# Fetching the blocks for a seven-product matrix multiply from ScalarE's queue instead of GpSimd's

## What is computed

```python
def _swiglu(x, w_gate, w_up, w_down):
    return (jax.nn.silu(x @ w_gate) * (x @ w_up)) @ w_down

h = _rmsnorm(x, ffn1_norm[layer])
x = x + 0.5 * _swiglu(h, ffn1_w_gate[layer], ffn1_w_up[layer], ffn1_w_down[layer])
```

## Time and profile before

| | us |
|---|---|
| median of 3 runs | 2193.39 (2192.85 to 2194.36) |
| profiled execution, its own time | 2189.33 |
| span of its trace | 2187.6 |
| PE busy | 2072.6 (95%) |
| DVE busy | 1447.6 (66%) |
| ACT busy | 1184.1 (54%) |
| POOL busy | 930.6 (43%) |

### The profile page before, as it was taken

One profiled execution on the slowest core, in us unless ns is written; L12 is line 12 of the kernel. 1 busy time (PEld: TensorE's weight loads), 2 busy tenths in 40 slices (PEclk: granted clock), 3 DMA queues, 4 the chain that ended last, 5 costly groups with the idle time before them and its releaser, 6 DMA issues.

```text
span 2187.6 us, 35091 instructions
## 1 busy us (share of the span) xinstructions
PE 2072.6 (95%) x11738; PEld 1800.8 (82%) x11738; DVE 1447.6 (66%) x2525; ACT 1184.1 (54%) x2186; POOL 930.6 (43%) x709
## 2 busy tenths in 40 slices
PE   8999999899999989889999899999999998989998
PEld 6878888798888879888887788888878887988886
DVE  6597854787652377776258789899777348767523
ACT  4566653566642356665244467777655335666422
POOL 2233451755643275664327701201254317565431
PEclk9999999999999999999999999999999999999999
DMA  5323263445533245554324422222454434555331
GB/s 172 109 93 94 78 221 90 151 173 180 184 116 96 78 151 173 174 169 130 98 86 165 125 68 81 77 78 83 131 177 159 154 96 135 192 173 173 124 96 67
DMA packets 83027, 282.78 MB, mean 129 GB/s; under 512 B 9225, under 2 KB 9481, under 8 KB 82417
## 3 DMA queue, kind: packets, MB, share of 16 engines
q1 hardware_dynamic: 51120, 182.08, 26.8%
q0 software_dynamic: 20096, 72.18, 9.9%
q10 hardware_dynamic: 11712, 27.27, 3.3%
HBM read 261.03 MB, written 18.89 MB: 128 GB/s over the span
## 4 chain that ended last, share of the span: by engine, by line
PE 57%; issue 15%; DVE 12%; POOL 11%; ACT 2%; DMA 2%; POOLq 1%; SPq 0%; DVEq 0%; ACTq 0%
PE bank L188 15%; PE bank L190 15%; PE bank L189 15%; PE bank L195 2%; PE bank L194 2%; POOL s_raw L817 2%; DMA w_raw<-stream 2%; POOL s_holes L817 2%; DVE w_lo L162 2%; POOL s_raw L818 2%; POOL s_holes L818 2%; PE bank L2226 1%; POOL s_holes L820 1%; POOL s_raw L820 1%; DVE t_lo L674 1%
## 5 line engine op out<-in xcount | busy, mean ns | idle before, releaser
L162 DVE TENSOR_TENSOR w_lo<-w_raw,w_hi 128x1024 fp32r<-128x1024 f32 (+1 forms) x337 | 464.0, 1392 | 332.0 <-ACT w_hi L157 329.1
L157 ACT ACTIVATE w_hi<-w_raw 128x1024 fp32r<-128x1024 f32 (+1 forms) x337 | 330.9, 984 | 387.7 <-PE bank L190 227.5
L188 PE MATMUL bank<-xn_hi,w_hi 128*128 128x512 f32 (+1 forms) x1192 | 434.8, 365 | 7.4 <-DVE h L670 4.0
L190 PE MATMUL bank<-xn_hi,w_lo 128*128 128x512 f32 (+1 forms) x1192 | 420.2, 353 | 0.0
L189 PE MATMUL bank<-xn_lo,w_hi 128*128 128x512 f32 (+1 forms) x1192 | 419.4, 352 | 0.0
L188 PEld LDWEIGHTS bank<-xn_hi,w_hi 128*128 128x128 f32 x1192 | 226.5, 190 | 38.9 <-DVE h L670 5.2
L190 PEld LDWEIGHTS bank<-xn_hi,w_lo 128*128 128x128 f32 x1192 | 226.0, 190 | 30.8
L189 PEld LDWEIGHTS bank<-xn_lo,w_hi 128*128 128x128 f32 x1192 | 226.6, 190 | 28.1 <-issue 2.6
L188 PE MATMUL bank<-t_hi,s_hi 128*128 128x256 f32 x648 | 190.8, 294 | 34.4 <-ACT snaps L559 24.9
L851 POOL TENSOR_TENSOR down_lo<-h,down_hi 128x512 fp32r<-128x512 f32 x66 | 112.3, 1706 | 239.8 <-ACT down_hi L611 239.8
L188 PE MATMUL bank<-down_hi,w_hi 128*128 128x512 f32 x528 | 206.3, 391 | 6.3 <-POOL down_lo L851 6.3
(11 more groups left out here) (492 smaller groups left out, 5063.7 us busy)
## 6 DMA issues: line engine op xcount, KB each, us to landing
w_raw<-stream SPq DMA_DIRECT2D x337, 512.0 KB, 3.7
s_raw<-stream POOLq DMA_DIRECT2D x54, 512.0 KB, 4.5
s_holes<-stream POOLq DMA_DIRECT2D x48, 512.0 KB, 4.8
spill_g<-gate_out ACTq DMA_DIRECT2D x16, 256.0 KB, 2.0
m_more<-spill_g POOLq DMA_DIRECT2D x3, 1024.0 KB, 12.0
s_first<-stream POOLq DMA_DIRECT2D x6, 512.0 KB, 4.5
x<-xt SPq DMA_DIRECT2D x4, 512.0 KB, 6.9
x<-xt ACTq DMA_DIRECT2D x1, 2048.0 KB, 10.8
```

What stands on the lines that cost most here:

```text
L157: nc.scalar.activation(w_hi[:, slot, at], w_raw[:, slot % 2, at], ACT.Copy).then_inc(split_hi, 1)
L162: nc.vector.tensor_tensor(w_lo[:, slot, at], w_raw[:, slot % 2, at], w_hi[:, slot, at], ALU.subtract).then_inc(split_lo, 1)
L188: nc.tensor.matmul(to, a_hi, b_hi, start=start, stop=False, skip_group_check=True)
L190: return nc.tensor.matmul(to, a_lo, b_hi, start=False, stop=stop, skip_group_check=True)
```

## The change

`raw_to` moves from GpSimd to ACT. ACT issues the two fetches of a tile at the end of its own work on a tile, behind silu, in a new step `third_raw`: it waits until the four low parts of the tile that the buffer holds are made, and then fetches the tile two further into the same buffer. GpSimd only waits for the data and makes sums. The fetches count in two semaphores of their own (`raw_in`, reused from the load of x at the start). ACT's loop over bodies ends one body earlier, and that body is written out, because the last tiles need no fetch. The first fetches of a layer stand in ACT's program behind the square root of the norm and in the third plain tile. The second copies of the high parts in PSUM stay.

```diff
-                def raw_to(i, q):
-                    for g in range(2):
-                        chunk = stream[4 * i + (first_in + gate_of(q) + g)]
-                        ...
-                def next_raw(i, q):
-                    pool.wait_ge(c["lo"], part_made("lo", i, q, 4))
-                    raw_to(i + 1, q)
...
+            def raw_to(eng, i, q):
+                for g in range(2):
+                    chunk = stream[4 * i + (first_in + gate_of(q) + g)]
+                    if q == 0 or (isinstance(i, int) and i == 0):
+                        to = (s_raw if q == 0 else s_first)[:, g].rearrange("p h w -> p (h w)")
+                        eng.dma_start(to, chunk).then_inc(raw_in[q], 16)
+                    else:
+                        eng.dma_start(s_holes[g][:, :, H:S], chunk.rearrange("p (k c) -> p k c", c=H)
+                                      ).then_inc(raw_in[q], 16)
...
+                def third_raw(i, q):
+                    of, to = {-1: ((i, 0), (i + 1, 0)), 0: ((i, 1), (i + 1, 1)), 1: ((i + 1, 0), (i + 2, 0))}[q]
+                    act.wait_ge(c["lo"], part_made("lo", *of, 4))
+                    raw_to(act, *to)
...
                 for q in range(2):
                     seven(0, q, True)
-                with act.Fori(1, BODIES - 1) as i:
+                    third_raw(0, q)
+                with act.Fori(1, BODIES - 2) as i:
                     for q in range(2):
                         seven(i, q, True)
+                        third_raw(i, q)
...
-                sums(0, 0)
-                sums(0, 1)
-                finished(pool, first_in, 2 * PLAIN - 1)
-                for q in range(2):
-                    next_raw(0, q)
-                    sums(1, q)
-                with pool.Fori(1, BODIES - 1) as i:
+                for i in range(2):
                     for q in range(2):
-                        next_raw(i, q)
-                        sums(i + 1, q)
+                        sums(i, q)
+                with pool.Fori(2, BODIES) as i:
+                    for q in range(2):
+                        sums(i, q)
```

More of the change, by code:

```diff
@@ L143, in build_program @@
         x_in, col_in = [sem(f"x_in{n}") for n in range(4)], sem("col_in")
+        raw_in = x_in[2:]
         passed = sem("passed")
@@ L303, in feed_forward @@
             pb = count_up(scaled=5 * SEVENS)["scaled"]
-            raw_loaded = list(gates_n)
-            for t in range(2):
-                gates_n[t] += 32 * BODIES
+            raw_loaded = 16 + 32 * BODIES * (ffns[0] - 1)
             def summed(i, q, n):
@@ L538, in act_part @@
                                      scale=1.0 / D).then_inc(m["root"], 1)
+                raw_to(act, 0, 0)
                 def silu_of(t, scaled):
@@ L584, in seven @@
                     if joint and q == 1 and more:
-                        if isinstance(i, int):
+                        if isinstance(i, int) and i == 0:
                             nc.scalar.activation(fin_r[:], x[:, 0, :], ACT.Square).then_inc(f["added"], 1)
@@ L599, in act_part @@
                             t_high(n, n)
+                    if t == 2:
+                        raw_to(act, 0, 1)
                     silu_of(t % 2, 2 * t + 2 * b + 1)
+                third_raw(0, -1)
                 for q in range(2):
                     seven(0, q, True)
-                with act.Fori(1, BODIES - 1) as i:
+                    third_raw(0, q)
+                with act.Fori(1, BODIES - 2) as i:
                     for q in range(2):
                         seven(i, q, True)
+                        third_raw(i, q)
+                for q in range(2):
+                    seven(BODIES - 2, q, True)
+                    if q == 0:
+                        third_raw(BODIES - 2, q)
                 for q in range(2):
@@ L798, in pool_part @@
                                             ALU.add).then_inc(m["added"], 1)
-                def raw_to(i, q):
-                    for g in range(2):
-                        chunk = stream[4 * i + (first_in + gate_of(q) + g)]
[L803 to L808, removed]
-                def next_raw(i, q):
-                    pool.wait_ge(c["lo"], part_made("lo", i, q, 4))
-                    raw_to(i + 1, q)
                 def sums(i, q):
-                    pool.wait_ge(gates_in[q], 32 * i + (raw_loaded[q] + 32))
+                    pool.wait_ge(raw_in[q], 32 * i + (raw_loaded + 32))
                     a11, a12, a21, a22 = (raw_of(n, i, q) for n in (S2, S4, S3, S1))
@@ L828, in pool_part @@
                 pool.wait_ge(m["added"], nb["added"] + KT - 1)
-                raw_to(0, 0)
                 nc.gpsimd.tensor_tensor(t1, b12, b11, ALU.subtract).then_inc(c["sum"], 1)
@@ L836, in pool_part @@
                 pool.wait_ge(c["sum"], c0["sum"] + 4)
-                raw_to(0, 1)
-                sums(0, 0)
-                sums(0, 1)
-                finished(pool, first_in, 2 * PLAIN - 1)
-                for q in range(2):
-                    next_raw(0, q)
-                    sums(1, q)
-                with pool.Fori(1, BODIES - 1) as i:
+                for i in range(2):
                     for q in range(2):
-                        next_raw(i, q)
-                        sums(i + 1, q)
+                        sums(i, q)
+                with pool.Fori(2, BODIES) as i:
+                    for q in range(2):
+                        sums(i, q)
                 def down_low(j, k):
```

## The result

The changed kernel takes 2214.05 us (2211.34 to 2216.02, median of 4 runs) against 2193.88 us for the kernel before beside it: a ratio of 1.0091, 95% interval 1.0073 to 1.0108. It is slower by 0.9%. The forecast was 2206 us in a range of 2172 to 2238, slower with a chance of 0.62. Sign and mechanism came out as forecast. In the sum two terms of the loop were too small, the collision was priced too high, the lower clock of TensorE had no term, and the layer start had its sign wrong. These errors partly cancel.

What follows compares the result with a forecast made beforehand. GpSimd's fetch and sums in series were taken to bound the later tiles (11.8 us against TensorE's 10.08). Adding 11.9 us for three layers and 0.8 for layer starts to 2193.4 gave 2206 us, range 2172 to 2238.

Steps and rivals of the forecast that it cites:

- the sum: Whole kernel: three layers at 594.9 us, 11.9 more than 583.0, plus 0.8 for layer starts; 2193.4 + 12.7 = 2206 us.
- the collision: DVE's norm lines wait for running GpSimd sums, so S3 low ends 1.3 us later, repeating each tile: 12.0 us.
- the layer start: First fetches on ACT at each layer's start: a loss of 0 to 1 us a layer, 0.8 in all.
- GpSimd's loop as the bound before, and its removal: Later tiles: GpSimd's fetch 5.22 and sums 6.55 us in series bound them; removing that gains at most 70.7 us.
- The new loop through S3 low, two DMAs, high part and snap: From one join of y to the next, through DVE, ACT and TensorE: 10.71 us a tile without sums interfering.
- ACT's wait, register steps and two DMAs: On ACT between S3 low and the high part: 1.45 us, with 0.9 from below and 2.0 from above.
- TensorE's stretch: TensorE's release, blocks three to six and DVE's release: 5.86 us of each tile.
- A cheaper issue gives back less than it saves: Faster DMA issue on ACT moves GpSimd's sums further into DVE's norm lines, so less returns than saved; no size given.
- The last interval of a layer: From tile 17 to tile 18 of each layer: taken as 9.5 us.
- What would show it: Profile signs: tiles of 11.7 to 12.3 us, one TensorE wait of nearly 2 us, two ACTq DMAs of 0.33 to 0.50.
- the signs for being wrong: TensorE waiting under 1 us a tile, DVE's norm lines undisturbed, or fetches landing so that sums lie elsewhere.
- The rule against the sum: Skill's rule that starting a DMA is usually small beside its transfer, so nothing counts on ACT; against 0.33 to 0.50 us.

Runs made afterwards that it cites:

- experiment 2: Changed kernel with GpSimd's sums cut to 8 of 256 columns and ACT's hardware loop over bodies written out in Python: 2123.32 us, ratio 0.9676.
- experiment 1: Changed kernel with each of GpSimd's four sums for a tile cut to 8 of 256 columns: 2141.79 us, ratio 0.9767.
- experiment 3: Changed kernel with only ACT's hardware loop written out, sums whole: 2199.37 us, ratio 1.0034.
- experiment 8: Changed kernel with ACT's two fetches issued ahead of silu, S3 low left behind the norm lines: 2224.10 us, ratio 1.0135.
- experiment 4: Changed kernel with 12 dummy matmuls ahead of TensorE's wait for block three: 2218.11 us, ratio 1.0111.
- experiment 5: Changed kernel with ACT's two fetches of a tile issued behind the last snap of the next tile: 2154.0 us, ratio 0.9826.
- experiment 6: Changed kernel with S3 low placed ahead of the two norm lines on VectorE, ACT's order kept: 2165.44 us, ratio 0.988.
- experiment 7: Changed kernel with S3 low ahead of the norm lines and ACT's two fetches ahead of silu: 2134.92 us, ratio 0.9732.
- experiment 9: Changed kernel with fetches behind the next tile's last snap and S3 low ahead of the norm lines: 2168.42 us, ratio 0.9874.
- experiment 11: Changed kernel with S3 low ahead of the norm lines, fetches ahead of silu and ACT's loop written out: 2127.30 us, ratio 0.9691.
- experiment 10: Kernel before with only the first two tiles' fetches of each layer issued by ACT: 2184.04 us, ratio 0.9962.

## Why the prediction was right or wrong

**GpSimd's loop as the bound before, and its removal: right.** POOL went from the chain and no longer waits for low parts.

**The new loop through S3 low, two DMAs, high part and snap: right in kind, 0.4 us short in size on average.** Two terms were too small, each read against the tile of experiment 2 and its sibling in experiment 1. "ACT's wait, register steps and two DMAs", taken as 1.45 us, is 1.7 inside the hardware loop and 1.58 over all middle tiles. I had priced the register steps by SP's records and left out ACT's loop and the high part's own steps. TensorE's stretch, taken as 5.86, is 6.11: from the snap's end at 465.60 to the join at 471.71. The first matmul after a wait has 0.22 to its successor instead of 0.12, and the join waits for the end of the last one, which lies 0.28 and not 0.12 behind its start. So the loop is 2.09 + 1.7 + 1.32 + 6.11 = 11.2 us, which experiment 1 shows. That experiment 2 comes to 10.70, the very 10.71 of the sum, is a coincidence: without the hardware loop ACT's term is below my 1.45 (0.95 and 1.4) by as much as TensorE's is above.

**The collision: right in kind, too dear.** Its place (sums starting 3.3 us ahead of the join) was seen at 2.8 to 4.4 in the 30 of 42 tiles that it hits. The other 12 all stand behind a tile of lower clock: their sums start 4.6 to 5.4 us ahead and are over in time, so the delay doesn't repeat each tile, as I had said. Its price of 1.3 us stands against 1.2 in the tiles hit and 0.86 over all. The 1.31 of experiment 1 (54.9 / 42) is near my 1.3 by luck, since it holds the lower clock too, for which I had no term.

**"A cheaper issue gives back less than it saves": open.** The edit of experiment 3 saves 16.3 us with the collision and 16.6 without it, but in the first figure 12 us more for the lock and 12 us less for the lower clock cancel.

**The sum.** I had 11.9 us more for the three layers and it is 31.4. The tiles' 12.0 instead of 12.41 is 42 x 0.4 = 17: the loop's missing 0.4 us and 0.45 for the lower clock, less 0.44 that the lock cost below its price. The last interval of a layer takes 10.08 and not 9.5 (1.7 in all), since I carried over 9.48 from the kernel before, where it began late (VectorE joined y of tile 17 at 622.09, and block seven had begun at 621.20); the first is 10.9 and not 10.7 (0.7).

**The layer start: sign wrong.** I put 0 to 1 us a layer as a loss. It is a gain of 8.1 us in all. I had looked at TensorE and at the wires there, and not at GpSimd, whose two DMA instructions (1.10 us at 526.18 in the earlier trace rows) also stood ahead of the sums that block VectorE there. This error partly cancels those of the tiles: the span grew by 23.0 us and not by 12.7. That 2206 lies only 8 us below the result is in part luck.

**What would show it.** The distance was to be 11.7 to 12.3 us; it is 10.9 to 14.3 with a mean of 12.41. One wait a tile at block three, ACT idle behind silu, two ACTq DMAs in the gap: all there. But of the signs for being wrong two came in some tiles, always behind one of lower clock: VectorE's pair ran undisturbed, or nearly, in 12 of the 42, and TensorE waited less than 1 us in 7. And ACT did wait for a sum at times (2.1 us in two waits in the first layer's middle tiles). The DMAs of 0.33 to 0.50 us hold for `s_raw`; those into `s_holes`, with rows of 1 KB, take 0.55 to 0.65.

**The rule against the sum.** The DMAs on ACT's queue hold it for 0.35 and 0.57 us each and stand in the chain with 3%. The Trainium skill, "DMA: Bandwidth & Descriptors", section on issuing engines, calls the time on the sequencer usually small beside the transfer. That is so here (4.2 us to landing), but on an engine in the loop it isn't the transfer that it must be held against.

## What to carry to other kernels

When work moves from an engine that was late to one that was idle on average, look at what it stands ahead of there, and put it into a wait that exists anyway. Here the same two DMAs cost 0.9% behind silu and, with the step that they wait for moved up, gained 2.7% ahead of it. Price an issue on a compute engine with its register steps and the loop's branch, and the restart of a stalled TensorE with its first and last matmul. When an engine loses an instruction, ask also what its other work now collides with, or no longer does.

## What the runs showed of the hardware

The granted clock fell to its lower level inside a busy loop. In the changed kernel this happened in 13 of 51 tiles, after TensorE had waited 1.9 to 2.6 us for the snap. It did in 5 tiles of experiment 3 (after 1.9 to 2.2 us) and in 13 of experiment 8 (after 1.9 to 2.3 us). Other tiles with waits as long kept the full clock: 9 of the changed kernel, 3 of experiment 3 and 15 of experiment 8. None of the 51 intervals of the kernel before (longest wait 1.39 us) or of experiments 1, 2, 4 to 7, 9 and 11 (at most 1.73 us) shows it, and none of experiment 10, with one wait of 1.99 us. In the changed kernel such a tile is followed by one of 10.9 to 11.5 us, whose sums are over, or nearly, before the join, so only 7.5 us of the loss stay.

Written out, ACT's addresses save 0.3 us per pair of fetches, and 0.7 where the loop's branch goes as well, between experiments 1 and 2. That is more than the records of the two lines add up to: at the medians shown 0.18 us for the four of a pair of fetches and 0.05 for the branch.
